# A two-layer mixture-of-experts block: shared expert's gate/up moved ahead of the expert loop, one expert kept in a spare room, a three-bank gather, a shorter routing chain

## The reference

```python
for layer in range(2):
    h = mixer(x)
    x = layer_norm(ALPHA * x + h)
    s = sigmoid(x @ router_w); sb = s + router_bias          # 64 experts in 8 groups
    # the 4 best of 8 groups by the sum of their two best experts, then the 6 best experts in them
    gate = s[chosen] / sum(s[chosen]) * 2.5
    routed = sum over the chosen e: gate_e * ((silu(x @ w_gate[e]) * (x @ w_up[e])) @ w_down[e])
    shared = (silu(x @ sh_gate) * (x @ sh_up)) @ sh_down     # hidden width 256, as each expert's
    x = layer_norm(ALPHA * x + routed + shared)
```

## Time and profile before

| | us |
|---|---|
| median of 3 runs | 1361.3 (1356.18 to 1366.25) |
| profiled execution, its own time | 1367.81 |
| its span | 1366.0 |
| TensorE busy | 1248.0 (91%) |
| mean DMA rate over the span | 325 GB/s |

### The profile page before, as it was taken

How to read it: one execution, slowest core, us unless ns; L and a number is a source line. 1 busy time by engine, 2 the same in 40 slices (tenths; PEclk the granted TensorE clock), 3 DMA queues, 4 the chain that set the end, 5 groups by cost and what they waited for, 6 DMA issues and landing times.

```text
span 1366.0 us, 15840 instructions
## 1 busy us (share of the span) xinstructions
PE 1248.0 (91%) x6183; PEld 570.7 (42%) x6183; DVE 366.1 (27%) x751; ACT 254.9 (19%) x532; POOL 16.0 (1%) x22
## 2 busy tenths in 40 slices
PE   7988988999999999999968898899999999999994
...
GB/s 334 190 191 87 1 193 196 421 421 421 422 346 424 421 421 399 421 420 422 423 284 93 275 1 165 145 421 422 420 422 412 356 421 421 396 421 421 421 421 106
DMA packets 67579, 444.52 MB, mean 325 GB/s; under 512 B 7616, under 2 KB 11968, under 8 KB 16192
## 3 DMA queue, kind: packets, MB, share of 16 engines
...
HBM read 442.59 MB, written 1.05 MB: 325 GB/s over the span
## 4 chain that ended last, share of the span: by engine, by line
PE 84%; DVE 7%; ACT 5%; issue 3%; DMA 1%; POOL 0%; POOLq 0%; DVEq 0%; SPq 0%
PE psum L660 33%; PE psum L680 17%; PE psum L623 5%; PE psum L772 4%; PE psum L531 4%; PE psum L706 4%; PE psum L559 2%; PE psum L692 2%; DVE room L1393 2%; PE psum L865 2%; PE psum L476 1%; ACT room L1008 1%; PE psum L891 1%; ACT arena L994 1%; PE psum L636 1%
## 5 line engine op out<-in xcount | busy, mean ns | idle before, releaser
L660 PE MATMUL psum<-ring,arena 128*64 128x512 f32 x2048 | 458.5, 600 | 12.4 <-issue 12.4
L660 PEld LDWEIGHTS psum<-ring,arena 128*64 128x64 f32 x2048 | 159.1, 138 | 300.5 <-issue 300.2
L680 PE MATMUL psum<-ring,room 128*64 128x512 f32 x1024 | 233.8, 598 | 4.1 <-ACT room L1015 1.8
L1402 DVE TENSOR_TENSOR y_low<-psum,y_high 128x1024 fp32r<-128x1024 f32 x64 | 78.4, 1224 | 354.2 <-ACT y_high L1001 354.2
L1393 DVE SCALAR_TENSOR_TENSOR room<-room,arena,psum 128x256 f32<-128x256 f32 x64 | 30.7, 480 | 370.9 <-ACT room L1008 370.9
L680 PEld LDWEIGHTS psum<-ring,room 128*64 128x64 f32 x1024 | 72.3, 136 | 133.7 <-issue 116.9
L1001 ACT CAST y_high<-psum 128x1024 fp32r<-128x1024 f32 x64 | 64.8, 1012 | 252.6 <-PE psum L680 252.6
L1008 ACT ACTIVATE room<-psum 128x256 f32<-128x256 f32 x64 | 24.6, 384 | 417.2 <-PE psum L660 417.2
L623 PE MATMUL psum<-onehot,x_high 128*128 128x256 f32 x256 | 76.6, 326 | 9.7 <-ACT arena L994 3.2
L706 PE MATMUL psum<-y_high,spread 32*128 32x512 f32 x512 | 65.0, 497 | 5.0 <-issue 4.9
L623 PE MATMUL psum<-onehot,x_low 128*128 128x256 f32 x256 | 66.3, 284 | 0.0
...
## 6 DMA issues: line engine op xcount, KB each, us to landing
ring<-in_expert_w_gate SPq DMA_DIRECT2D x128, 1024.0 KB, 13.1
ring<-in_expert_w_up SPq DMA_DIRECT2D x128, 1024.0 KB, 15.2
ring<-in_expert_w_down SPq DMA_DIRECT2D x128, 1024.0 KB, 15.1
...
```

Source lines behind the costliest of these rows:

```text
L660: mm = pe.matmul(BANK[2][CAP * e:CAP * e + CAP, :], xg[:, c, 2 * j + e, :], expert(slot[j % NPAIR * 2 + e])[0][:, c], start=c == 0, stop=c ...
L680: mm = pe.matmul(PS[0][CAP * e:CAP * e + CAP, half * 512:(half + 1) * 512], ht[:, c, CAP * e:CAP * e + CAP], expert(slot[j % NPAIR * 2 + e ...
L1402: V.tensor_tensor(ylo, PS[0][:, :], yhi.bitcast(F32), ALU.subtract).then_inc(sem[f"yd_dve{L}"], 1)
```

## The change

1. The shared gate/up weights are loaded into the arena's attention scratch as soon as the last attention product is done (`pv_pe`), not into the room of `w_out`. Both chunks' shared gate/up products come ahead of the loop (in banks 4 and 5), and so do their transposes (bank 6, `pe_shared_turns`, behind the first `pe_slots`); the extra step at group 3 is gone. The shared down product is moved from group 5, j = 0, to group 2, j = 2, behind that pair's gate/up.
2. Expert 63 is loaded once into the room of `w_out` (`keep`) when the output product is done, and the last pair reads it there. Slot 3 is not refilled in the last round: 59 refilled experts instead of 60. The vectors of the second norm now go into slot 1, behind a wait for the down product of pair 30, no longer right behind the last refill.
3. The gather takes turns between banks 0, 1 and 2; its third chunk waits for the hidden rows of the pair at hand (`h_dve`), whose gate/up stands in bank 2.
4. From the output product on, the order is woven (`pe_mixed`, `mixed`, `act_mixed`): transposes of chunk 0 between the two column halves of chunk 1's output product, its residual sum in halves, and pieces of the shared gate/up between the steps of the router.
5. Routing has fewer steps: one mask step instead of two, one masking sum instead of a product and a sum (2 instructions fewer), one rank step instead of two; `pe_rank` waits for `sel` and no longer for the gates, whose five instructions come behind it.
6. For layer 1, `q_norm`, `kv_norm` and `w_out` are loaded when the accumulators of layer 0 are done, no longer after its last norm.

```diff
-        norm = dict(mix=(lnp[:, 0:D], lnp[:, D:2 * D]), ffn=(wbig[:, 0:D], wbig[:, D:2 * D]))
+        norm = dict(mix=(lnp[:, 0:D], lnp[:, D:2 * D]), ffn=(slot[1][:, 4096:4096 + D], slot[1][:, 4096 + D:SLOT]))
+        keep = wbig[:, 0:SLOT]
...
-        shared_down = wbig[:, 4096:4096 + DE // P * D]
+        shared_up = arena[:, 4096:4096 + 2 * KC * DE]
+        shared_down = xt
...
         def refills(sp, L):
-            n_rounds = pass_groups(sp) * GP // NPAIR
-            with sp.Fori(0, n_rounds - 1) as i:
+
+            n_rounds = pass_groups(sp) * (GP // NPAIR)
+
+            def refill(i, kept=None):
                 for j in range(NPAIR):
+                    mine = [k for k in (2 * j, 2 * j + 1) if k != kept]
                     sp.wait_ge(sem[f"gu_pe{L}"], (i * NPAIR + j + 1) * 2)
-                    for k in (2 * j, 2 * j + 1):
+                    for k in mine:
                         expert_gate_up(sp, L, k, ((i + 1) * NSLOT + k) % NE)
                     sp.wait_ge(sem[f"down_pe{L}"], (i * NPAIR + j + 1) * 2)
-                    for k in (2 * j, 2 * j + 1):
+                    for k in mine:
                         expert_down(sp, L, k, ((i + 1) * NSLOT + k) % NE)
 
+            with sp.Fori(0, n_rounds - 2) as i:
+                refill(i)
+            refill(n_rounds - 2, NSLOT - 1)
+            sp.wait_ge(sem[f"down_pe{L}"], n_rounds * 4 - 2)
+            norm_loads(sp, "ffn", ln_ffn_g, ln_ffn_b, L)
+
         def mixture_loads(sp, L):
 
-            sp.wait_ge(sem["out_pe"], TC * (L + 1))
-            load_gate_up(sp, wbig, s_gate[L], s_up[L], sem["shared_in"])
+            sp.wait_ge(sem["pv_pe"], (BOTH["pv_pe"], BOTH["pv_pe"] + len(UNITS[1]))[L])
+            load_gate_up(sp, shared_up, s_gate[L], s_up[L], sem["shared_in"])
             sp.dma_start(mcon, moe_const).then_inc(sem["moec_in"], 16)
-            load_expert(sp, L, 3, 3)
+            expert_gate_up(sp, L, 3, 3)
+            if L == 0:
+                expert_down(sp, L, 3, 3)
+            sp.wait_ge(sem["out_pe"], BOTH["out_pe"] * (L + 1))
+            if L:
+                expert_down(sp, L, 3, 3)
+            load_gate_up(sp, keep, e_gate[L, NE - 1], e_up[L, NE - 1], sem["keep_gu_in"])
+            load_down(sp, keep, e_down[L, NE - 1], sem["keep_dn_in"])
+            sp.wait_ge(sem["sgu_pe"], TC * (L + 1))
             sp.dma_start(shared_down, s_down[L].rearrange("(p c) n -> p (c n)", c=DE // P)).then_inc(sem["shdown_in"], 16)
             sp.wait_ge(sem["groups_dve"], L + 1)
             refills(sp, L)
-            sp.wait_ge(sem["sgu_pe"], TC * (L + 1))
-            norm_loads(sp, "ffn", ln_ffn_g, ln_ffn_b, L)
...
-            with eng.Fori(1, SHARED_UP) as i:
+            with eng.Fori(1, SHARED_DOWN) as i:
                 group(i, False)
-            for i in range(SHARED_UP, SHARED_DOWN + 1):
-                group(i, False)
+            group(SHARED_DOWN, False)
...
-            return isinstance(i, int) and i == step and j == 0
+            return isinstance(i, int) and i == step and j == 2
...
-                if c >= 2:
-                    pe.wait_ge(sem[f"{'xg_dve' if c % 2 else 'xg_act'}{L}"], i * 4 + c // 2)
-                got = BANK[c % 2].rearrange("p (e u s) -> p e u s", e=GE, u=TC)
+                if c >= 3:
+                    before = c - 3
+                    pe.wait_ge(sem[f"{'xg_dve' if before % 2 else 'xg_act'}{L}"], i * 4 + before // 2 + 1)
+                if p is None and c == 4:
+                    pe.wait_ge(sem[f"xlo_dve{L}"], 3)
+                if p is not None and c == 2:
+                    pe.wait_ge(sem[f"h_dve{L}"], p + 1)
+                got = BANK[c % 3].rearrange("p (e u s) -> p e u s", e=GE, u=TC)
...
+            stored = [slot[j % NPAIR * 2 + e] for e in range(2)]
             for e in range(2):
-                pe.wait_ge(sem[f"gu{j % NPAIR * 2 + e}_in{L}"], (turn + 1) * 32)
+                if last and j == GP - 1 and e:
+                    stored[e] = keep
+                    pe.wait_ge(sem["keep_gu_in"], BOTH["keep_gu_in"] * (L + 1))
+                else:
+                    pe.wait_ge(sem[f"gu{j % NPAIR * 2 + e}_in{L}"], (turn + 1) * 32)
...
-                    if shared_step(i, j, SHARED_UP):
-                        pe.wait_ge(sem[f"h_dve{L}"], p)
-                        pe_shared_up(pe, L, 1)
-                        pe_combine(pe, L, p - 1, before, 0)
-                        pe.wait_ge(sem[f"ht_act{L}"], p)
-                        pe_shared_turn(pe, L, 0)
-                        pe_combine(pe, L, p - 1, before, 1)
-                        pe_shared_turn(pe, L, 1)
-                        pe_gate_up(pe, L, i, j)
-                        pe_turn(pe, L, p, i + 1)
-                        pe_down(pe, L, i, j, last)
-                        continue
+                    pe_gate_up(pe, L, i, j, last)
                     if shared_step(i, j, SHARED_DOWN):
                         for tc in range(TC):
                             pe_shared_down(pe, L, tc)
-                    pe_gate_up(pe, L, i, j)
...
-        def pe_moe_steps(pe, L):
-            pe_shared_up(pe, L, 0)
+        def pe_mixed(pe, L):
+
+            st = 1 + 2 * L
+            pe.wait_ge(sem["o_dve"], (L + 1) * BOTH["o_dve"])
+            pe_out_part(pe, L, 1, range(KC))
+            pe_columns(pe, st, 0, "lnmix_dve", TC * L)
+            pe_out_part(pe, L, 1, range(KC, 2 * KC))
+            pe_logits(pe, L, 0)
+            pe_shared_up(pe, L, 0, range(3))
+            pe_columns(pe, st, 1, "lnmix_dve", TC * L)
+            pe_shared_up(pe, L, 0, range(3, 4))
+            pe_logits(pe, L, 1)
+            pe_shared_up(pe, L, 0, range(4, KC))
+            pe_shared_up(pe, L, 1, range(4))
             pe_rank(pe, L)
+            pe_shared_up(pe, L, 1, range(4, KC))
             pe_experts(pe, L)
...
+        def act_mixed(act, L):
+
+            st = 1 + 2 * L
+            act_x_high(act, L, 0, slice(0, KC))
+            for b in range(3):
+                tc, c = b // 2, b % 2 * 4
+                if b == 2:
+                    act_x_high(act, L, 1, slice(0, 4))
+                act.wait_ge(sem["xt_pe"], 4 * st + b + 1)
+                nc.scalar.copy(xcol[:, c:c + 4, tc * P:(tc + 1) * P], v(BANK[b], c=4, t=P)).then_inc(sem["xt_act"], 1)
+            act_x_high(act, L, 1, slice(4, KC))
+            act_logits(act, L)
+            act_moe(act, L)
...
+            def mixed(L):
+
+                def summed(tc, half):
+                    dve.wait_ge(sem["out_pe"], L * BOTH["out_pe"] + tc * 2 + half + 1)
+                    cols = slice(half * 512, (half + 1) * 512)
+                    r = xrow[:, tc, cols]
+                    link(V.scalar_tensor_tensor(r, r, ALPHA, OUT[tc][:, cols], ALU.mult, ALU.add))
+                    link(V.bn_stats(stats[:, 6 * half:6 * half + 6], r))
+
+                summed(0, 0)
+                summed(0, 1)
+                dve.wait_ge(sem["ln_mix_in"], 32 * (L + 1))
+                normed(0, "mix")
+                settle("lnmix_dve")
+                summed(1, 0)
+                x_low(L, 0, slice(0, KC))
+                summed(1, 1)
+                normed(1, "mix")
+                x_low(L, 1, slice(0, 4))
+                columns(1 + 2 * L)
...
-                link(V.tensor_scalar(gsel, gpick[:, :, 0:NG], PICKED / 2, None, ALU.is_ge))
-                link(V.tensor_scalar(gneg, gsel, 1.0, -NEG, ALU.subtract, ALU.mult))
+                link(V.tensor_scalar(gneg, gpick[:, :, 0:NG], PICKED / 2, -NEG, ALU.is_lt, ALU.mult))
                 for tc in range(TC):
                     e3 = v(esc[:, tc, 0:NE], g=NG, k=EPG)
-                    V.tensor_tensor(e3, v(rsb[:, tc, :], g=NG, k=EPG), gsel[:, tc, :, None].to_broadcast([P, NG, EPG]), ALU.mult).then_inc(sem["dve_chain"], 1)
-                    chain[0] += 1
-                dve.wait_ge(sem["dve_chain"], chain[0])
-                for tc in range(TC):
-                    e3 = v(esc[:, tc, 0:NE], g=NG, k=EPG)
-                    ins = V.tensor_tensor(e3, e3, gneg[:, tc, :, None].to_broadcast([P, NG, EPG]), ALU.add)
+                    ins = V.tensor_tensor(e3, v(rsb[:, tc, :], g=NG, k=EPG), gneg[:, tc, :, None].to_broadcast([P, NG, EPG]), ALU.subtract)
...
-                link(V.tensor_scalar(sel, epick[:, :, 0:NE], PICKED / 2, None, ALU.is_ge))
+                mark(V.tensor_scalar(sel, epick[:, :, 0:NE], PICKED / 2, None, ALU.is_ge), "sel_dve")
+                settle("sel_dve")```

**On TensorE, from the last attention product to the ranks** (L531 and L548 of the change are the output product, L438/L455 the transposes, L548/L559 the logits, L559/L571 the shared gate/up, L569/L583 the ranks). Before:

```order
L510 MATMUL psum<-arena 64x256 x4
L531 MATMUL psum<-room 128x512 x16
L438 MATMUL psum<-cst,x_rows 128x128 x8
L548 MATMUL psum<-rw,room 128x64 x8
L438 MATMUL psum<-cst,x_rows 128x128 x8
L548 MATMUL psum<-rw,room 128x64 x8
L559 MATMUL psum<-room 128x512 x8
L569 MATMUL psum<-arena 128x64
```

189 lines of the change are left out of this document (90 added, 99 removed).

## The result

| | before | changed |
|---|---|---|
| median, us | 1361.8 (1356.2 to 1366.3, 4 runs) | 1338.7 (1335.1 to 1343.4, 4 runs) |
| ratio to before | | 0.983 (0.980 to 0.985) |
| profiled execution: own time / span, us | 1367.8 / 1366.0 | 1341.2 / 1339.4 |
| TensorE busy, us | 1248.0 | 1221.3 |
| mean DMA rate, GB/s | 325 | 332 |

Faster by 1.7%, and the whole interval lies beyond the 1% set ahead. The forecast was 1336, the range 1326 to 1349.

A forecast was written before the change was run, and what follows sets the result against it. Loads were taken to bind the expert loops, a chain across engines the transitions. Gains of 2 x (2.8 + 9.7) = 25 us take the span from 1366.0 to 1341, the median to 1336; range 1326 to 1349.

The forecast's parts named there:

- Loads bind the loop: Expert loop: a group of four needs 55.0 us on TensorE against 59.8 of loads, so loads bind.
- The standing bus was the cost: Expert loop: loads stood still 7.5 us per layer, nearly all at group 3; regained, gate/up 30 comes at 439.9.
- I give its gate/up the 8.78 of rows 4: Pair 30: after waiting about 2 us, its gate/up takes the slow 8.78 us, so the pair takes 14.4.
- term 2: Expert loop to the end of gate/up 31: 9.7 us gained per layer, 11.4 if pair 30 keeps full clock.
- 0.5 later than TensorE wants it: Loop's end: a 60th refill would arrive at 454.8, 0.5 us late, so the kept expert alone is worth little.
- The transition: Output product to first gate/up: 2.8 us gained per layer, from full clock, shorter routing and a faster gather.
- TensorE is late, not the choice: Transition: expert choice done at 200.8, TensorE's eight shared matmuls only at 201.7, so the ranks wait for TensorE.
- Rival A: Transition: the clock falls at gaps around the second transposes; its gain becomes -0.7 per layer, 1343 us; chance 0.15.
- gaps under 1 us did no harm: Transition: gaps of 0.7 to 0.8 us had left the clock at 1.00, so full clock was assumed.
- C: Expert loop: waits for loads slow every pair's gate/up, TensorE binds; 1397 us, slower; chance 0.05.
- The gather: Ahead of gate/up: three banks instead of two save 1.9 us per gather, with bounds from nothing to 1.9.
- B: Expert loop: loads keep standing still, at pair 10 or an unseen stall, costing 7.5 us again; 1351; chance 0.11.

The follow-up runs named there:

- r_two_banks: The changed kernel with the gather back on two banks instead of three; 1341.6 us.
- r_idle_gap: The changed kernel with three shared gate/up matmul pairs moved from in front of chunk 1's transposes to behind them; 1343.7 us.
- r_copies_first: The changed kernel with both engines' copies of chunk 1's transposes put ahead of x's high and low parts; 1335.3 us.
- r_both: The changed kernel with the copies first, as in r_copies_first, and expert 59 kept instead of 63; 1331.9 us, ratio 0.977.

## Why the prediction was right, step by step

**Loads bind the loop: shown.** TensorE's own need up to gate/up 30 was put at 417 us; with fewer bytes to load it was 419.2. The two-bank run shows the reverse side: more work on TensorE, same loop.

**The standing bus was the cost: shown in size, and in two parts.** Gate/up 30 was forecast at 439.9 and came at 440.3 and 440.1. The 7.5 us were split rightly (6.1 and 1.4): the two variants of the kernel before recover part of each, in their windows. What the prediction did not see is that the step's cost was not its products alone: with seven eighths of them gone 2.9 of the 6.1 stayed, for gate/up 12 stood behind its combines and transposes as well, and the wait that opened between them was followed by 1.35 us of lost clock. The shared down product at pair 10 cost nothing, as said: the window over it (224 to 450) is at 421.

**Gate/up 30 and 31: the term was too small by 1.3 and 1.9.** The step that failed is "I give its gate/up the 8.78 of rows 4". Pair 30 waited 0.26 us in layer 0 (pair 27 had taken the slow gate/up, which used up TensorE's lead) and 1.92 in layer 1, and took 7.1 both times. So term 2 is 11.0 and 11.6, not 9.7; the value in brackets there, 11.4, was the better one. With the pair at full clock TensorE wants expert 63 at 453, not at 454.3, and a 60th refill, forecast to arrive at 454.8, arrives at 455.1: the kept expert saves 2.2 to 2.3 of waiting and 1.7 of slow gate/up. "0.5 later than TensorE wants it" was the same error seen from the other side.

**The transition: 2.8 forecast, 3.3 and 1.7 measured.** Counted from the start of the output product, the steps of layer 0 came close to their forecast: second logits at 22.8 (22.9), choice done at 31.0 (31.1), TensorE free at 31.6 (32.0), first gather at 35.5 (36.4), gate/up 0 at 41.3 (41.9). "TensorE is late, not the choice" held, by half a us. Of the 3.3 some 1.6 is the first gather (r_two_banks); of the woven order only one piece was taken back (r_idle_gap), and no run takes back the earlier loads. In layer 1 the clock fell behind the 0.97 us gap, for the one stretch from 836.7 to about 840, and that costs 1.7. Rival A was thus half right in that layer: it named the gaps on both sides of the second transposes, and the clock did fall behind the second of them; but the logits kept the clock of 1.00, only the shared matmuls behind them lost, and the price was 1.7, not 3.5. The step that failed is "gaps under 1 us did no harm": in the profiles of the changed order, 9 of 16 transitions have the eight shared matmuls at 8.78 in place of 7.08, 2 of 8 in layer 0 and 7 of 8 in layer 1, with the same gap in each. Where no gap is left (r_copies_first, r_both), 4 of 4 have 7.09. That the gap is needed for the fall is thus well supported, though four are few; why layer 1 is hit more often is open. The Trainium skill (TensorE: Matmul & The Clock Gate, section HAM oscillation) tells of bursts that each start at the half clock behind waits for DMA of some 3 to 5 us. The gap here is 0.97 and the waits ahead of gate/ups are about 2, so by that section neither would cost anything, and the trace disagrees: both were followed by the half clock in part of the cases. The prediction's "by that rule the time is C's" read the section too widely for waits of 2 us.

**The gather**: 1.6 per gather in the two-bank run, 1.9 forecast. TensorE's idle time ahead of gather products is 9.7 us in all in the kernel before and 0.0 now, so the banks were what it waited for. In the sum it counts once per layer.

**Rivals B and C** are out: no slice of the page is under 420 in the stream (the lowest window above has 419), and of 13 waits of 1.9 us or more ahead of a gate/up, five were followed by 8.78 and eight by 7.09. A slow one costs the loop nothing while loads bind, for the next wait is shorter by as much: pair 7 takes 8.78 in layer 0 and 7.09 in layer 1, pair 10 then waits 0.19 and 1.90, and the rate stays at 421. The 1.5 us that the prediction would add to term 2 at the 358 GB/s of the Trainium skill (DMA: Bandwidth & Descriptors, section Where 436 GB/s comes from) is an estimate that comes to 1.3 when redone (7.5 x 421/358 = 8.8); at the 421 measured it does not arise.

**The norm's vectors** landed in 5.3 us, not 11:

```profile
ring<-in_ln_ffn_b SPq DMA_DIRECT2D x2, 512.0 KB, 5.3
```

They were issued at 664.9 as gate/up 31 began, on an idle bus, and the residual sum ahead of the norm began 17.6 us later (682.5).

**The sum** was 25 against 26.6 of span: transition +5.0 where 5.6 was said, loop +22.6 where 19.4 was said, about -1 elsewhere. The loop's error and the transition's are of opposite sign, both about which gate/up or stretch gets the half clock, so that the sum is nearer than its terms is in part luck. In medians the gain is 23.1 where 25 was forecast.
